# Projection products beside memory heads and state-space steps: one lot per step instead of two

## What is computed

```python
def even_mixer(x, w_in, b_in, ml_norm, w_out):          # layer 0
    u = x @ w_in + b_in
    mq, mk, mv, mo, mi, mf, fq, fk, fv, ff = split_sizes(u, ...)
    h_ml = mlstm_chunkwise(heads(mq, 4), heads(mk, 4), heads(mv, 4), mi, mf)   # memory heads
    h_ml = sigmoid(mo) * head_norm(h_ml, ml_norm)
    h_fx = forgetting_attention(heads(fq, 8), heads(fk, 8), heads(fv, 8), ff)
    return concatenate([h_ml, h_fx]) @ w_out

def odd_mixer(x, w_in, ...):                            # layer 1
    z, xbc, dt_raw, pool_in = split_sizes(x @ w_in, ...)
    ...
    y = ssd_chunked(xh * dt, dt * a, bm, cm)            # state-space steps
    y = rms_norm((y + d_skip * xh) * silu(z), ssm_norm)
    return concatenate([y, multiscale_pool(pool_in, ...)]) @ w_out
```

## Time and profile before

| | |
|---|---|
| median of 3 runs | 2175.53 us (2174.11 to 2177.61) |
| profiled execution, its own time | 2177.96 us |
| its span in the profile | 2176.2 us |
| PE busy | 2133.0 us, 98% of the span |
| DVE busy | 1282.4 us, 59% |
| ACT busy | 916.8 us, 42% |
| granted TensorE clock, mean | 0.995 of full |
| memory heads (first e to first logits) | about 102.3 to 174.2 us of the span |
| state-space steps | about 746.6 to 805 us of the span |

### The profile page before, as it was taken

One profiled execution on the slowest core, in us unless ns is written; L12 is line 12 of the kernel. 1 busy time (PEld: TensorE's weight loads), 2 busy tenths in 40 slices (PEclk: granted clock), 3 DMA queues, 4 the chain that ended last, 5 costly groups with the idle time before them and its releaser, 6 DMA issues.

```text
span 2176.2 us, 26662 instructions
## 1 busy us (share of the span) xinstructions
PE 2133.0 (98%) x10600; PEld 1730.0 (79%) x10608; DVE 1282.4 (59%) x1965; ACT 916.8 (42%) x1549; POOL 101.1 (5%) x155
## 2 busy tenths in 40 slices
PE   8999999999999999999999999999999999999998
PEld 7866688888888758888888878777787888888887
DVE  6445475555437767655543749456777657555534
ACT  4135553334326556333342642354444645333421
POOL 0000031000000003200000000000012200000000
PEclk9999999999999999999999999999999999999999
DMA  5312123333322203332333322212222023333332
GB/s 202 95 59 78 51 95 97 97 97 116 97 87 98 77 30 118 98 97 96 117 98 95 124 80 88 78 29 79 87 72 74 2 78 99 96 98 97 117 97 76
DMA packets 50954, 194.00 MB, mean 89 GB/s; under 512 B 5648, under 2 KB 5648, under 8 KB 49808
## 3 DMA queue, kind: packets, MB, share of 16 engines
q1 hardware_dynamic: 50832, 192.30, 27.7%
HBM read 188.09 MB, written 4.19 MB: 88 GB/s over the span
## 4 chain that ended last, share of the span: by engine, by line
PE 89%; DVE 5%; ACT 4%; issue 1%; DMA 0%; ACTq 0%; DVEq 0%
PE bank L398 27%; PE bank L400 26%; PE bank L399 26%; PE bank L972 2%; PE bank L698 1%; ACT arena L1250 1%; DVE small L1868 1%; PE bank L676 1%; ACT whi L1145 1%; PE bank L687 0%; PE bank L613 0%; DVE arena L1986 0%; DVE xs L1863 0%; PE bank L770 0%; PE bank L942 0%
## 5 line engine op out<-in xcount | busy, mean ns | idle before, releaser
L398 PE MATMUL bank<-xs,whi 128*128 128x512 f32 (+2 forms) x1992 | 772.0, 388 | 12.9 <-DVE xs L2202 7.5
L400 PE MATMUL bank<-xs,wlo 128*128 128x512 f32 (+2 forms) x1992 | 751.2, 377 | 0.0
L399 PE MATMUL bank<-xs,whi 128*128 128x512 f32 (+2 forms) x1992 | 750.8, 377 | 0.0
L1842 DVE TENSOR_TENSOR wlo<-ring,whi 128x1024 fp32r<-128x1024 f32 x333 | 415.3, 1248 | 295.8 <-ACT whi L1145 295.5
L1145 ACT ACTIVATE whi<-ring 128x1024 fp32r<-128x1024 f32 x333 | 350.7, 1055 | 261.2 <-DMA ring<-stream 261.1
L398 PEld LDWEIGHTS bank<-xs,whi 128*128 128x128 f32 x1992 | 376.2, 189 | 96.9 <-issue 12.2
L400 PEld LDWEIGHTS bank<-xs,wlo 128*128 128x128 f32 x1992 | 375.8, 189 | 69.8
L399 PEld LDWEIGHTS bank<-xs,whi 128*128 128x128 f32 x1992 | 376.4, 189 | 67.5 <-issue 2.9
L398 PE MATMUL bank<-whi,xs 128*128 128x512 f32 (+1 forms) x808 | 315.4, 390 | 2.0 <-issue 2.0
L399 PE MATMUL bank<-wlo,xs 128*128 128x512 f32 (+1 forms) x808 | 312.0, 386 | 0.0
L400 PE MATMUL bank<-whi,xs 128*128 128x512 f32 (+1 forms) x808 | 312.0, 386 | 0.0
(11 more groups left out here) (363 smaller groups left out, 1766.5 us busy)
## 6 DMA issues: line engine op xcount, KB each, us to landing
ring<-stream SPq DMA_DIRECT2D x333, 512.0 KB, 3.6
arena<-gains SPq DMA_DIRECT2D x5, 1024.0 KB, 5.6
arena<-xt SPq DMA_DIRECT2D x4, 512.0 KB, 6.0
arena<-xn SPq DMA_DIRECT2D x1, 2048.0 KB, 8.6
kept<-arena SPq DMA_DIRECT2D x1, 2048.0 KB, 7.2
arena<-kept SPq DMA_DIRECT2D x1, 2048.0 KB, 8.1
out<-arena SPq DMA_DIRECT2D x4, 512.0 KB, 2.6
con<-consts SPq DMA_DIRECT2D x1, 744.0 KB, 11.3
```

What stands on the lines that cost most here:

```text
L398: nc.tensor.matmul(out, ah, bh, start=first, stop=False)
L399: nc.tensor.matmul(out, ah, bl, start=False, stop=False)
L400: return nc.tensor.matmul(out, al, bh, start=False, stop=last)
L1842: V.tensor_tensor(wlo[:, v % SLOTS, :], ring[:, v % SLOTS, :], whi[:, v % SLOTS, :], ALU.subtract).then_inc(wlo_done, 1)
```

## The change

Both slot loops issue their projection products in one lot per slot (memory heads) or per two steps (state-space). In `mlstm` the second lot, which stood behind P·V and `head_norms`, joins the first, behind s(n) and ahead of P·V. In `ssd` the even steps from 2 on have no product any more; the odd step issues its own and those of the even step before it, all ahead of its P·V. No matmul is added or removed, no bank or buffer is another, and the instructions of DVE, ACT, POOL and SP are the same in the same order.

```diff
-        ml_pieces = [[(beside_ml[i // DC], i % DC) for i in range(DC * len(beside_ml) * x // (2 * ML_SLOTS), DC * len(beside_ml) * (x + 1) // (2 * ML_SLOTS))]
-                     for x in range(2 * ML_SLOTS)]
-        ml_evacuate = {x // 2 + 1: unit for x in range(2 * ML_SLOTS) for unit, k in ml_pieces[x] if k == DC - 1}
+        ml_pieces = [[(beside_ml[i // DC], i % DC) for i in range(DC * len(beside_ml) * x // ML_SLOTS, DC * len(beside_ml) * (x + 1) // ML_SLOTS)] for x in range(ML_SLOTS)]
+        ml_evacuate = {x + 1: unit for x in range(ML_SLOTS) for unit, k in ml_pieces[x] if k == DC - 1}
...
-                    for j, k in z_pieces.get(n, ())[:1]:
+                    for j, k in (z_pieces[0] if n == 0 else (z_pieces.get(n - 1, []) if n > 1 else []) + z_pieces.get(n, []) if n % 2 else ()):
                         z_piece(j, k)
                     if n % 2 and n >= 5:
...
-                    for j, k in z_pieces.get(n, ())[1:]:
-                        z_piece(j, k)
...
-                    for (name, i), k in ml_pieces[2 * n]:
+                    for (name, i), k in ml_pieces[n]:
                         piece(name, i, k)
...
                     head_norms(n)
-                    for (name, i), k in ml_pieces[2 * n + 1]:
-                        piece(name, i, k)
```

## The result

| | before | changed |
|---|---|---|
| median of 16 runs each | 2178.05 us | 2182.45 us |
| lowest and highest | 2174.11 to 2179.12 | 2179.18 to 2183.29 |
| profiled execution: own time, span | 2177.96, 2176.2 us | 2180.93, 2179.1 us |

The ratio is 1.0020, 95% interval 1.0014 to 1.0027: the change costs 4.4 us, 0.2%. The forecast was 2177.9 us, with 2180.6 as the upper end of its range. Of the 16 executions of the changed kernel, nine have a mean granted clock of 0.993, lower than either profiled execution (0.995 both); its median is one of them.

A forecast was written before the change was run, and what follows sets the result against it. PE was taken to bound the kernel, busy for 98% of the span. Terms -0.3 + 1.2 + 1.3 - 0.6 + 0.8 = +2.4 us on 2175.53 gave 2177.9 us, range 2174.4 to 2180.6 us.

The forecast's parts named there:

- waits A: Memory heads, slot 13: PE waits 1.2 us for bank 4 before the first product of fk unit 2; bounds 0.9 and 1.4.
- wait B: Second pair of logits: PE waits 1.3 us for bank 0, released by DVE L2050; bounds 1.1 and 1.5.
- wait C: State-space step 13: e(13) waits 0.8 us for bank 3, held until ACT does w(11); bounds 0.4 and 1.1.
- from L795's start ... 3.72 us, without a gap: Slot 12: ACT's chain from the floor of head 2 to the release of bank 4 takes 3.72 us.
- The cover of "0.1 to 0.2 us at best" for bank 0: Second pair of logits: slack between L2050's end at 174.84 and PE's claim of bank 0 at 175.00.
- the two old waits behind B: Denominator and mean square of head 3: PE's existing waits of 1.51 and 0.99 us move whole, catching none of the 1.3 us.
- the savings: Fewer switches between kinds of matmul: 0.3 us in the memory heads, 0.6 us in the state-space steps.
- the covers priced at nothing: Other moves of P·V and norms, bank releases in slots 4 to 10 and fq units: priced at 0.
- the median the sum was put on: Forecast base: 2175.53 us, 2.4 us below the profiled execution's 2177.96, giving 2177.9 us with +2.4.
- The clock: Rival: further stretches at 1.2 GHz add 1.6 us each, with two 5.6 us, 2181.1; chance of at least two 0.12.
- Covers hold: Rival: A, B and C absent since ACT's chain is less tight; only savings stay, -0.9 us, 2174.6; chance 0.14.
- half of it: Rival: one of A and B appears, or the second is swallowed; +1.1 us, 2176.6; chance 0.12.

The follow-up runs named there:

- the heads with the read first: Memory heads alone changed, with ACT's split and read of the finished fk unit ahead of the norms' floor and root: 2176.72 us, ratio 0.9999 against before.
- the one with the norms' matmuls late: Kernel before, both lots and P·V in place, only floor, denominator and mean square moved behind the second lot: 2179.21 us, ratio 1.0013.
- the state-space part alone: Kernel before with only the state-space steps changed to one lot per two steps, memory heads as before: 2177.12 us, ratio 0.9998.
- the third profile of the change: Whole change, unaltered, timed a third time: 2181.04 us, ratio 1.0025 against before; the profiled execution had a mean clock of 0.993.
- the second profile of the change: Whole change, unaltered, timed again beside other kernels on one chip: 2181.24 us, ratio 1.0020 against before.
- the whole with the read first: Whole change, with ACT's split and read of the finished unit ahead of the norms' work: 2177.04 us, ratio 1.0000 against before.
- the long lot behind: Memory heads with one lot per slot, placed behind P·V and the norms' matmuls, state-space steps as before: 2177.64 us, ratio 0.9999 against before.
- the heads alone: Kernel before with only the memory heads changed to one lot per slot, timed twice: 2179.76 us, ratio 1.0010, and 2181.19 us, ratio 1.0021.

## Why the prediction missed, by its own steps

**Right: waits A, B and C.** Places, releasing lines and sizes. By starts, as the prediction worked them out, they cost 1.33, 1.40 and 0.90 us against 1.2, 1.3 and 0.8; in brackets the profile has 1.08, 1.32 and 0.74. The step "from L795's start ... 3.72 us, without a gap" held to 0.01 us. (In the sum for wait C, 766.64 + 0.58 is 767.22, not 767.25; its 0.8 us stands.) The cover of "0.1 to 0.2 us at best" for bank 0 was none. That the two old waits behind B move as a whole held too. The kernel with the read first shows the cause by taking it away, the one with the norms' matmuls late by putting it into before.

**Right: the savings.** State-space some 0.8 us against 0.6, within its bounds. What the prediction worked out from the Trainium skill (TensorE: Matmul & The Clock Gate, section "Architectural detail: the array is 16× 32×32, not 1× 128×128"), that PE's queue can pull weight loads ahead of matmuls in flight, does not hold at every switch here: the saving would then be 0, and the state-space part alone would be 0.90 us later where it is 0.09. What the switch costs its 0.06 us for, no run shows. In the memory heads 0.3 us is there by 152.2 us (0.82 to 0.51), and 0.4 at their end: 1.33 + 1.40 - 0.4 makes the 2.33 us that were found.

**Right: the covers priced at nothing.** No other wait has come up, and everything from 200 to 745 us is later by 1.9 to 2.1 us beyond the start-up's 0.82, where 2.2 was said.

**Wrong: the median the sum was put on.** "The median of the runs is 2.4 us lower; on it, 2175.53 + 2.4 = 2177.9." The three runs shown had a median of 2175.53; sixteen have 2178.05, and three groups of 23 to 33 have 2177.4 to 2177.6. The profiled execution's own 2177.96 us was the better base: 2180.4 on it. The table shows why three runs are too few: executions of one kernel at 0.995 and 0.997 are 3.5 us apart, more than the whole sum. The range should have been laid about both bases. This is over half of the miss of 4.5 us.

**Wrong: the clock as a rival only.** "It decides from the second stretch on ... Chance of at least two 0.12." Both sides of that sentence were off. A stretch was treated as there or not, and the forecast, with at most one, had nothing in its sum for it; what was to be priced was a share of executions. With 13 of 35 executions of the change at 0.993 and 5 at 0.996 or 0.997, it is 1.5 to 2.0 us in the mean. The reason given, idle time just ahead of a place whose clock already fell, fits the third profile of the change, where the clock falls behind wait B. The row held against it, "after 0.9 us of idle time in the state-space steps the clock stayed at 1.00", compared one wait of 0.90 us among full work with 1.32 us that has 1.51 and 0.99 more within 6 us of it. 5.6 us behind the stretch that was read, the profile of before has two waits close together, and there its clock does fall:

```profile
793.56 0.28 PE L589 MATMUL bank<-arena 72*128 72x256 bf16 x1 [1.47 <-ACT arena L1400]
...
794.55 0.28 PE L589 MATMUL bank<-arena 72*128 72x256 bf16 x1 [0.65 <-ACT arena L1400]
```

From 795 to 800 us it is 0.66 in the mean. In the second profile of the change the same two waits are there and the clock stays at 1.00 from 788 to 806. The sentence of the Trainium skill (TensorE: Matmul & The Clock Gate, section "What's actually happening") that the throttled state is the default and activity releases it fits these counts: ten more matmuls in place of the idle time, and no execution of 22 at 0.993.

**The rivals.** "Covers hold" and "half of it" are out: both waits are there in every profile of the change. "The clock" gave 2181.1 for two stretches, on a base that was 2.5 us low; as a mechanism it holds for the 13 of 35 executions at 0.993.

With 2178.05 as the base, 2.4 us of waits and 1.5 to 2.0 of clock, the sum is 2181.9 to 2182.5 us, where 2182.45 was measured. This is no test of the account, since the clock term is taken in part from the same executions.

No version beats the kernel before: the heads with the read first, the whole with the read first, the long lot behind and the state-space part alone have 0.9998 to 1.0000 with intervals across 1.

## What to carry to other kernels

Before a matmul is moved behind others, follow what it feeds through the in-order lists of the other engines: here a row of 0.35 us of slack, not visible as any wait, stood between a moved floor and a bank whose read is four instructions further down ACT's list, and moving the independent read ahead of the dependent one removes the wait at no cost that was seen. Where two waits are short, measure them from start to start as well, since the idle time in brackets leaves out part of them. Where engines are full, compare the length of each shift with the slack of the next claim, place by place. Effects of a few us in two thousand need a base of many runs, sorted by the clock of each execution, and a term for what a change does to the mix of clocks.

## What the hardware showed that was not expected

The same kernel on the same chip has executions at mean clocks 0.995, 0.996 and 0.997 with 2178.1, 2176.9 and 2174.6 us. Low stretches come and go at fixed places: the start of the attention had 3.4 us at 0.50 in the profile of before and in the first of the change, 6.8 and 10.2 us in the second and third, and none in either of the heads alone, of which the first reads

```profile
177.00:184.00 7.00, 3.76 (x15) 1.70 (x16) 4.71 (x12) 1.76 (x6) 0.00 (x0) 1.00 0.45 154
```

with waits A and B as long as in the change (and 1.00 from 184 to 192 as well). Over all thirteen profiles: of the six with waits A and B, three have no low stretch at this place and three have 3.4, 6.8 and 10.2 us; of the seven without, three have none and four have 3.4. So the idle time does not decide it for one execution, but the two long stretches stand only where it is. One profile of a kernel therefore does not tell its clock.

Within a long lot the product matmuls close up. In the timeline of PE in slot 16 of the changed kernel

```profile
173.18 0.40 PE L398 MATMUL bank<-xs,whi 128*128 128x512 f32 x1
...
173.65 0.39 PE L397 MATMUL bank<-xs,whi 128*128 128x512 f32 x1
...
175.46 0.39 PE L399 MATMUL bank<-xs,wlo 128*128 128x512 f32 x1
```

the first two steps are 0.235 us each and the next eight 0.226. It may be where part of the 0.31 us of the first slots comes from; no run took it apart.
